# A hybrid encoder step on one core: projections, attention and convolution done per block of 384 rows

## What is computed

```python
xn = rmsnorm(x, norm1_g)
z  = xn @ w_in                      # conv B | conv C | conv h | q | k | v | two gates, 8192 columns
a  = (B * dwconv3_causal(C * h)) @ w_conv_out
q, k = rope(rmsnorm(q)), rope(rmsnorm(k))          # 8 heads, two components of 64
o  = (softmax(q1 k1^T / 8) - lam * softmax(q2 k2^T / 8)) @ v   # chunk-causal; sample rows see 1024 cached keys
b  = (rmsnorm(o) * 0.8) @ w_attn_out
x  = x + (sigmoid(gA) * a + sigmoid(gB) * b) @ w_o
# PEER: per row 8 heads x 16 experts out of 16384, chosen by two top-16 searches over 128 keys
h  = gelu(u[e] . xn2);  x = x + sum_e softmax_weight(e) * h(e) * v[e]       # 128 pairs of rows u, v per row of x
```

## Time and profile before

| | us |
|---|---|
| median of 3 runs | 4466.34 (4462.66 to 4469.68) |
| the profiled execution, its own time | 4468.1 |
| its span | 4466.3 |
| PE busy in the span | 3853.3 (86%) |
| DVE busy | 2490.5 (56%) |
| ACT busy | 1451.2 (32%) |
| POOL busy | 1441.8 (32%) |
| DMA, mean over the span | 295 GB/s, 1318.22 MB |
| granted TensorE clock, mean | 0.967 |

### The profile page before, as it was taken

How to read it: one execution, slowest core, us unless ns; L and a number is a source line. 1 busy time by engine, 2 the same in 40 slices (tenths; PEclk the granted TensorE clock), 3 DMA queues, 4 the chain that set the end, 5 groups by cost and what they waited for, 6 DMA issues and landing times.

```text
span 4466.3 us, 43158 instructions
## 1 busy us (share of the span) xinstructions
PE 3853.3 (86%) x12044; PEld 2048.3 (46%) x12044; DVE 2490.5 (56%) x5795; ACT 1451.2 (32%) x4313; POOL 1441.8 (32%) x1429
## 2 busy tenths in 40 slices
PE   7989999899798899898878998988897777777877
PEld 6657566575455544444434444334453222222222
DVE  4443544435100387767656666666665666666664
ACT  2221312213101244433334444333433333333333
POOL 3112120121000144334444344444444444444442
PEclk9999999999899999999989999999999999999999
DMA  5111011100533699999999999999999999999998
GB/s 176 49 59 48 27 53 47 49 24 21 148 103 111 237 420 415 395 419 403 413 398 419 420 420 419 412 420 420 386 389 417 421 419 420 417 408 413 414 415 343
DMA packets 265946, 1318.22 MB, mean 295 GB/s; under 512 B 28960, under 2 KB 91936, under 8 KB 130400
## 3 DMA queue, kind: packets, MB, share of 16 engines
q0 software_dynamic: 154816, 1116.82, 60.8%
q1 hardware_dynamic: 102000, 175.81, 11.5%
q10 hardware_dynamic: 8880, 22.68, 1.3%
HBM read 1271.17 MB, written 44.06 MB: 294 GB/s over the span
## 4 chain that ended last, share of the span: by engine, by line
DMA 31%; PE 27%; DVE 7%; issue 3%; ACT 3%; POOL 1%; DVEq 1%; ACTq 0%; SPq 0%; POOLq 0%
PE tl_ps L1206 16%; DMA tl_ringx<-in_peer_uv,tl_idx 15%; DMA mix<-in_peer_uv,tl_idx 15%; PE tl_ps L1155 5%; PE tl_ps L1191 3%; PE tl_ps L1167 2%; DVE tl_ringx L1507 2%; DVE mix L1507 2%; ACT tl_dg L1315 1%; PE tl_ps L1135 1%; ACT tl_hw L1308 1%; POOL mix L1096 1%; POOL tl_ringx L1096 0%; ACT tl_hg L1304 0%; DVE tl_oh L1421 0%
## 5 line engine op out<-in xcount | busy, mean ns | idle before, releaser
L1206 PE MATMUL tl_ps<-mix,tl_dg 128*128 128x512 f32 x2296 | 1124.9, 618 | 236.9 <-ACT tl_dg L1315 215.5
L1507 DVE CUSTOM_DVE_ANT_0 mix<-mix,tl_xb 128x1024 f32<-128x1024 f32 x604 | 738.8, 1225 | 570.4 <-DMA mix<-in_peer_uv,tl_idx 554.8
L1096 POOL DMA_INDIRECT mix<-in_peer_uv,tl_idx x604 | 690.9, 1144 | 951.2 <-PE tl_ps L1206 775.3
L1206 PE MATMUL tl_ps<-tl_ringx,tl_dg 128*128 128x512 f32 x1712 | 845.8, 622 | 169.5 <-ACT tl_dg L1315 158.7
L1206 PEld LDWEIGHTS tl_ps<-mix,tl_dg 128*128 128x128 f32 x2296 | 420.2, 194 | 818.4 <-ACT tl_dg L1315 462.4
L1507 DVE CUSTOM_DVE_ANT_0 tl_ringx<-tl_ringx,tl_xb 128x1024 f32<-128x1024 f32 x452 | 552.8, 1225 | 404.0 <-DMA tl_ringx<-in_peer_uv,tl_idx 388.1
L1304 ACT ACTIVATE tl_hg<-tl_hd 128x1 f32<-128x1 f32 x1056 | 213.8, 202 | 1635.7 <-DVE tl_hd L1507 1622.1
L1096 POOL DMA_INDIRECT tl_ringx<-in_peer_uv,tl_idx x452 | 517.0, 1144 | 700.7 <-PE tl_ps L1206 573.9
L1206 PEld LDWEIGHTS tl_ps<-tl_ringx,tl_dg 128*128 128x128 f32 x1712 | 313.3, 194 | 615.2 <-ACT tl_dg L1315 344.9
L1315 ACT ACTIVATE tl_dg<-ident,tl_hw 128x128 f32<-128x128 f32 x1002 | 402.2, 401 | 82.8 <-PE tl_ps L1206 11.7
L1155 PE MATMUL tl_ps<-tl_xr,low 128*128 128x384 f32 (+1 forms) x1280 | 413.0, 454 | 2.8 <-issue 1.7
(11 more groups left out here) (170 smaller groups left out, 3057.2 us busy)
## 6 DMA issues: line engine op xcount, KB each, us to landing
low<-in_wall SPq DMA_DIRECT2D x168, 512.0 KB, 20.7
mix<-in_w_in SPq DMA_DIRECT2D x12, 1024.0 KB, 6.1
low<-in_w_in SPq DMA_DIRECT2D x24, 512.0 KB, 4.1
mix<-in_peer_uv,tl_idx POOLq DMA_INDIRECT x604
sc_rows<-tl_stage ACTq DMA_DIRECT2D x36, 256.0 KB
tl_sch<-sc_rows POOLq DMA_DIRECT2D x18, 512.0 KB, 13.2
tl_ringx<-in_peer_uv,tl_idx POOLq DMA_INDIRECT x452
xn_t<-xnT SPq DMA_DIRECT2D x1, 4224.0 KB, 21.7
```

Source lines behind the costliest of these rows:

```text
L1096: nc.gpsimd.indirect_dma_start(out=ring[q % RING].rearrange("p a d -> p (a d)"), out_offset=None, in_=A["peer_uv"], in_offset=bass.Indirec ...
L1206: last = nc.tensor.matmul(acc[:, h * 512:(h + 1) * 512], dg[:, npe(q) % DIAGS, :], ring[q % RING][:, 1, h * 512:(h + 1) * 512], start=k == ...
L1507: nc.vector.tensor_tensor_reduce(out=ring[q % RING][:, 0, :], in0=ring[q % RING][:, 0, :], in1=xb[:, t % 2, :], scale=1.0, scalar=0.0, op0 ...
```

## The change

`build_attention` is gone. Its work is done in `build_tail`, per block of rows, by a new generator `attend(rb)` on each engine, between that block's neighbours: `attend(0)` and `middle(0)` run in front of slot 0; `attend(1)` is due in slots 0 to 145 and `middle(1)`, now with the convolution of its rows, in 146 to 308; `attend(2)` in 312 to 497 and `middle(2)` with its convolution in 501 to 703. A head's step has 21 positions and a pace (`ATT`: 1.0, 0.78 and 0.98 slots a position), and `SC`, `PJ`, `TW`, `PV`, `TO`, `TQ` are the positions of its scores, projections (of the next head), transposes of weights, products with v and transposes of outputs and heads on PE. ACT's, DVE's and POOL's steps stand some tenths of a position to two positions behind. A projection is now 384 columns wide (q, k and v of one head at once). A block of rows attends to its own keys, which are in SBUF, and to prior ones, which are loaded from memory (`kt`, `v_prompt`; the cache's keys come transposed from the host). Rows that DVE adds are now 111 (`SHARED`: every second slot in 146 to 317, every third in 494 to 701).

```diff
+WRING = 6
 QUAD = 4
 DIAGS = 4
 
 
 BLOCKS = ((0, 3 * P, (0, 1, 2)), (3 * P, 3 * P, (3, 4, 5)), (6 * P, 2 * P + DEC, (6, 7, 8)))
 MID = 56
-START = -140
-PLAN = ((-137.2, 1600, 1600, 7), (-5.5, 1600, 780, 7), (262, 1, 420, 7))
-DVE_TO, DVE_EVERY = 256, 4
+START = -330
+ATT = ((-327.5, 1.0), (-2.5, 0.78), (312, 0.98))
+PLAN = ((-137.2, 1600, 1600, 7), (145, 1, 1750, 7), (499, 1, 1080, 7))
+SC, PJ, TW, PV = (0, 6, 12), (2.2, 8.2, 14.2), (3.4, 9.4, 15.6), (4.8, 10.8, 17)
+TO, TQ, CV = (7.2, 13.2, 19), (10.9, 16.6, 20), (0.6, 6.6, 12.8)
+CONV = (0, 24, 24)
+BASE = (0, MID, 2 * MID + 24)
+SHARED = ((146, 318, 2), (494, 702, 3))
 
 
 def rows_of(t):
...
-            sp.dma_start(keep["kc"][:], group_cols(A["cache_k"], 0)).then_inc(s["ahead"], 16)
-            for kind in range(3):
-                sp.dma_start(keep["w"][kind][:], group_cols(A["w_in"][0], (QCOL, KCOL, VCOL)[kind])).then_inc(s["ahead"], 16)
-            sp.wait_ge(s["ahead"], 64)
+            for k in range(6):
+                src = A["watt"][k] if k < 3 else A["wall"][k - 3]
+                sp.dma_start(keep["low"][:, k * D:(k + 1) * D], src).then_inc(s["ahead"], 16)
...
-def build_attention(nc, A, keep):
...
+def step_at(rb, h, pos):
+
+    first, pace = ATT[rb]
+    return first + ((h + 1) * 21 + pos) * pace
...
+                def project(g, i):
...
+                    for c in range(DC):
+                        yield PJ[i] + 0.1 * c
+                        if c == 0:
+                            if i == 0:
+                                seen = g + 1 if rb == 0 else DC * (1 - par) + 4 * (rb - 1) + g % DC // 2 + 1
+                                pe.wait_ge(s[f"a_in{par}"], 48 * seen)
+                            if j >= 2:
+                                pe.wait_ge(s["qn_d"], j - 1)
+                                pe.wait_ge(s["v_cp"], j - 1)
+                            if rb:
+                                pe.wait_ge(s["ex_d"], done["scores"])
+                        last = nc.tensor.matmul(o, xn[:, c, i * P:i * P + n], w[:, :, c, :], start=(c == 0), stop=(c == DC - 1))
+                    last.then_inc(s["pj_done"], 1)
+                    done["heads"] += 1
...
+                    for i, t in enumerate(tiles):
+                        if h >= 0:
+                            yield step_at(rb, h, SC[i])
+                            score(g, i, (0,) if t == NT else (0, 1))
+                            if rb == 0:
+                                for pos in conv_block(h, i):
+                                    yield step_at(rb, h, pos)
+                            if i:
+                                yield step_at(rb, h, TO[i - 1])
+                                turn_out(g, i - 1)
+                            if t == NT:
+                                yield step_at(rb, h, SC[i] + 1.6)
+                                score(g, i, (1,))
+                        if h + 1 < DC:
+                            for pos in project(g + 1, i):
+                                yield step_at(rb, h, pos)
+                        if h >= 0:
+                            blocks = (key_count(t) + P - 1) // P
+                            yield step_at(rb, h, TW[i])
+                            turn_weights(g, i, 0, blocks if turns(t) == 1 else 4)
+                            if turns(t) == 2:
+                                yield step_at(rb, h, TW[i] + 0.6)
+                                turn_weights(g, i, 4, blocks)
+                        if h + 1 < DC and i == 2:
+                            yield step_at(rb, h, TQ[1])
+                            turn_heads(g + 1, 1)
+                        if h >= 0:
+                            yield step_at(rb, h, PV[i])
+                            weigh_values(g, i)
+                        if h + 1 < DC and i == 1:
+                            yield step_at(rb, h, TQ[0])
+                            turn_heads(g + 1, 0)
+                    if h >= 0:
+                        yield step_at(rb, h, TO[2])
+                        turn_out(g, 2)
+                    if h + 1 < DC:
+                        yield step_at(rb, h, TQ[2])
+                        turn_heads(g + 1, 2)
...
+                    act.wait_ge(s["pj_done"], j + 1)
+                    nc.scalar.copy(Vown[:n, par, i, :], ps[:n, 2 + j % 2, 2 * P:3 * P]).then_inc(s["v_cp"], 1)
+                    if j:
+                        act.wait_ge(s["ss_d"], j)
+                    nc.scalar.activation(sq[:n], ps[:n, 2 + j % 2, 0:2 * P], ACT.Square, scale=HD ** -0.5).then_inc(s["sq_d"], 1)
...
+                    for i, t in enumerate(tiles):
+                        if h >= 0:
+                            if i:
+                                yield step_at(rb, h, TO[i - 1] + 0.2)
+                                keep_out(g, i - 1)
+                            if t == NT:
+                                yield step_at(rb, h, SC[i] + 1.4)
+                                exp_scores(g, i, (0,))
+                                yield step_at(rb, h, SC[i] + 2.9)
+                                exp_scores(g, i, (1,))
+                            else:
+                                yield step_at(rb, h, SC[i] + 1.5)
+                                exp_scores(g, i, (0, 1))
+                            if i == 0 and rb == 0:
+                                yield step_at(rb, h, CV[0] + 1.0)
+                                act.wait_ge(s["f_done"], 3 * h + 1)
+                                if h:
+                                    act.wait_ge(s["u_done"], h)
+                                nc.scalar.copy(Cb[:, 0:nr], ps[:, 6, 0:nr]).then_inc(s["c_done"], 1)
+                        if h + 1 < DC:
+                            yield step_at(rb, h, PJ[i] + 0.9)
+                            keep_value(g + 1, i)
+                        if h >= 0:
+                            for half in range(turns(t)):
+                                yield step_at(rb, h, TW[i] + 0.2 + 0.6 * half)
+                                keep_weights(g, i, half)
+                        if h + 1 < DC and i:
+                            yield step_at(rb, h, TQ[i - 1] + 0.2)
+                            keep_heads(g + 1, i - 1)
+                        if h >= 0:
+                            yield step_at(rb, h, PV[i] + 0.5)
+                            square_out(g, i)
+                    if h >= 0:
+                        yield step_at(rb, h, TO[2] + 0.2)
+                        keep_out(g, 2)
+                    if h + 1 < DC:
+                        yield step_at(rb, h, TQ[2] + 0.2)
+                        keep_heads(g + 1, 2)
+                        yield step_at(rb, h, TQ[2] + 0.6)
+                        store_heads(g + 1)
...
+                    for i, t in enumerate(tiles):
+                        if h >= 0:
+                            if i:
+                                yield step_at(rb, h, PV[i - 1] + 1.8)
+                                norm_out(g, i - 1)
+                            yield step_at(rb, h, SC[i] + 0.6)
+                            row_max(g, i, (0,) if t == NT else (0, 1))
+                            if t == NT:
+                                yield step_at(rb, h, SC[i] + 2.2)
+                                row_max(g, i, (1,))
+                            if rb == 0 and i:
+                                yield step_at(rb, h, CV[i] + 1.1)
+                                conv_product(h) if i == 1 else conv_taps(h)
+                            yield step_at(rb, h, SC[i] + (3.3 if t == NT else 2.4))
+                            difference(g, i)
+                        if h + 1 < DC:
+                            yield step_at(rb, h, PJ[i] + 1.2)
+                            mean_square(g + 1, i)
+                            yield step_at(rb, h, PJ[i] + 2.2)
+                            rotate(g + 1, i)
+                    if h >= 0:
+                        yield step_at(rb, h, PV[2] + 1.8)
+                        norm_out(g, 2)
...
-            steps = [started(middle(rb)) for rb in range(PASSES)] + [started(routing())]
+            steps = [started(part(rb)) for rb in range(PASSES) for part in (attend, middle)] + [started(routing())]
```

More of the change, by code:

```diff
@@ L835, in by_dve @@
 def by_dve(q):
-    return q < DVE_TO and (4 if q < SLOTS else 30) <= q % SLOTS < SLOTS - 4 and q % DVE_EVERY == DVE_EVERY - 1
+    t, k = divmod(q, SLOTS)
+    if not (4 if t == 0 else 30) <= k < SLOTS - 4:
+        return False
+    return any(first <= q < end and q % turn == turn - 1 for first, end, turn in SHARED)
 def ndve(q):
@@ L858, in slot_of @@
         return at / (ahead if at < 0 else rate)
-    for j in range(MID):
+    for j in range(-conv, MID):
         if j == 40:
@@ L1209, in weigh @@
                 last.then_inc(s["used_pe"], 1)
-            steps = [started(middle(rb)) for rb in range(PASSES)]
+            steps = [started(part(rb)) for rb in range(PASSES) for part in (attend, middle)]
             for q in range(START, LAST):
@@ L1341, in _ @@
```

(2 more changed lines are left out.)

1166 lines of the change are left out of this document (560 added, 606 removed).

## The result

The changed kernel takes 4766.5 us (median of 4 runs, 4761.5 to 4773.9) against 4468.0 (4 runs): ratio 1.067, 95% interval 1.065 to 1.069. It is slower, as forecast (4576 us, +2.4%), but by more than twice the forecast, and outside the range of 4310 to 4740.

A forecast was written before the change was run, and what follows sets the result against it. PE was taken to bound slots 0 to 703, gathers the rest: 771 + 466 + 230 + 638 + 33 + 569 + 273 + 638 + 41 + 906 + 11 = 4576 us; own range 4450 to 4700, over the cases 4310 to 4740.

The forecast's parts named there:

- First dot, 771: In front of the slots: first dot at 44.6 + 357 + 370 = 771 us, 771 earlier; bounds 720 and 830.
- The two middle stretches, 671 and 679: Slots 146 to 311 and 498 to 703: PE's work 638 us each, plus 33 and 41 at 0.2 a slot.
- The gathers alone, 906 and 11: From slot 704 on: 352 slots at the gathers' 2.574 us, 906 us as now, plus 11 at the end.
- The waits, 230 and 273: Attention slots 0 to 145 and 312 to 497: PE waits on ACT's same-iteration steps and exps, 503 us in all.
- Plain couplings: Attention slots: 84 and 91 iterations where PE waits for ACT's step and diagonal chain, mean 1.75 us, 147 and 159.
- Waits behind an exp: Attention slots: table loads and exps hold PE 5.3 us, or 2.4 with half a projection between; 83 and 114 us.
- VectorE joins in: Rival, chance 0.17: DVE's softmax and rotation add waits in the attention slots, 503 becomes 650; 4723 us.
- Transfers: Rival, chance 0.04: DMA sets the slots throughout, with PE under 2.8 us a slot; 3878 us.
- PE's own work, 466 and 569: Slots 0 to 145 and 312 to 497: PE's matmuls, 452 and 552 us at gapless prices, become 466 and 569.
- the clock of 0.97: Slots 0 to 703: PE's granted clock, taken from the kernel before, turning its priced work into 2311 us.
- two signs: Forecast wrong if PE's diagonal waits in the attention slots total under 390 us, or the first dot is beyond 830.
- absorbed: Rival, chance 0.29: ACT runs ahead in the attention slots, so waits are mostly absorbed, under 393 us; 4334 us.

The follow-up runs named there:

- experiment 1: Changed kernel with ScalarE doing slot q's gelu, gate and diagonal ahead of its attention and middle steps of the iteration; 4660.5 us, ratio 1.042.
- experiment 6: Changed kernel with TensorE doing slot q - 1's product in iteration q, behind its steps, instead of slot q's; 4441.2 us, ratio 0.992 to the kernel before.
- experiment 8: Kernel of experiment 6 with the exponentials replaced by a Square without a table, masked scores 0, so no softmax; 4364.6 us, ratio 0.976.
- experiment 3: Changed kernel with two zero-weight matmuls of 512 columns on TensorE before the diagonal wait in 230 attention iterations; 4822.4 us, ratio 1.078.
- experiment 4: Changed kernel with block 1's attention also in front of the gathers, its middle still at slots 145 to 311; 4831.7 us, ratio 1.080.
- experiment 5: Kernel of experiment 4 with three zero-weight matmuls of 512 columns ahead of each of 21 projection waits for an exp; 4785.4 us, ratio 1.070.
- experiment 2: Changed kernel with the attention's exponentials replaced by a Square needing no table of its own, masked scores 0, so no softmax; 4611.3 us, ratio 1.032.
- experiment 9: Kernel of experiment 6 with projections 0.8 of a position later, weight transposes and product with V 0.2 to 0.5 later; 4418.2 us, ratio 0.990.
- experiment 7: Kernel of experiment 6 with every fourth row of the attention stretches (66 more) added by VectorE; 4452.1 us, ratio 0.995.
- experiment 10: Kernel of experiment 9 with every fourth row of the attention stretches (66 more) added by VectorE; 4429.7 us, ratio 0.991.

## Why the forecast had the sign right and the size wrong

**First dot, 771.** It came at 779.9. Both of its parts are right as well: the first matmul of the merge (L978) starts at 413.2 us where 401.6 was forecast, and from there to the dot it is 367 us where 370 was.

**The two middle stretches, 671 and 679.** They took 652 and 683. Right; here the granted clock is 0.98 and 0.96, as assumed.

**The gathers alone, 906 and 11.** 931, 14 more; DMA's share is 0.99.

**The waits, 230 and 273.** They were 215 and 245. The mechanism is shown by experiments 1 and 6, which take the coupling away from either side. That the sum is so near is in part luck, since its two parts miss in opposite directions. Plain couplings were forecast at 84 and 91 waits of 1.75 us, 147 and 159 us; there were 61 and 74 of 1.5 us, 92 and 114. Waits behind an exp were forecast at 83 and 114 us; with those at L798 and L776 they came to 113 and 117. "VectorE joins in" is refuted, since all waits stayed under 503 and PE's own on DVE were 2.6 us in block 1 and 8.8 in block 2. Transfers did not set the pace (DMA's share 0.62 and 0.64).

**PE's own work, 466 and 569: the step that failed.** The prediction took the prices of gapless stretches and "the clock of 0.97" for stretches into which it had itself just put 503 us of waits. PE was busy 541 and 715 us, 75 and 146 more. With the other terms that is the miss: 9 + 75 - 15 - 19 + 146 - 28 + 4 + 14 = 186, and 4762.7 - 4576 = 187. These 221 us are of two kinds, and the trace's clock tells them apart. The low clock cost 50 and 97 us; the forecast's 0.97 held 14 and 17 of that, so 116 are clock that it left out. The other 106 are under-pricing: at full clock PE's work is 491 and 619 us, where the forecast had 452 and 552. Experiments 6 and 8, at higher clocks and with fewer waits, both give 478 and 607, so this count hangs little on the clock of the run. Of the 106 some 62 are in attention's scores, transposes and products with V (261 us for 199), 34 in the slots' products (596 for 562) and 9 in the projections. That the waits bring the low clock is shown by experiment 3 (78 us less for the same work with PE kept busy in the same waits) and by the pair 4 and 5.

The Trainium skill (TensorE: Matmul & The Clock Gate, HAM oscillation — how this bites in real kernels) describes just this, matmuls that start cold again after each wait, for a kernel that waits on DMA. The traces agree: 7.99 us against 5.43 for the same eight matmuls. The prediction did not weigh that page.

**The exponentials.** Forecast as the dearest waits for their number, 5.3 us behind most of them, 83 and 114 us in all. Experiment 2 puts the table loads that they bring at 155 us, 86 of it as waits and 69 as PE's busy time. In the changed kernel's first attention stretch (records, busy us, mean ns):

```profile
L1247 ACT ACT_TABLE_LOAD x27 | 34.6, 1283 | 0.5
L1058 ACT ACT_TABLE_LOAD x24 | 30.8, 1283 | 22.5 <-DVE tl_nb L1418 22.1
```

The loads are 1283 ns each, as forecast. The Trainium skill (ScalarE: Activation LUTs, What ACT_TABLE_LOAD costs) has 1.38 us of drain beside each; in block 2 an exp starts at 2619.99, 1.29 us after its load began at 2618.70, so the drain does not show here either.

**What would have shown it wrong.** The prediction named two signs. The first dot passed. The other, waits on diagonals under 390 us in the attention slots, came true: they were 182 + 198 = 380. Yet this does not make the rival "absorbed" right, which had the same bound (393) for all waits: those were 460, and the time was 430 us above its 4334. The sign counted diagonals alone, where the term of 503 held every wait, also those at L798 and L776. And no sign named PE's busy time or its clock, the term that failed.

Where the change goes wrong, then, is mostly in the order within an iteration. With that mended (experiments 6 and 9) the same restructuring is 0.8 and 1.0% faster than the kernel before. Open remains what sets the 4.0 and 4.15 us a slot that attention still takes in experiment 9. Experiment 7 excludes the amount of PE's work. The waits left there are 95 us on diagonals, 59 at L798 and L776 for exps, and smaller ones on DVE; which of these chains comes first was not shown, and banks of its own for the projection were not tried.

## What to carry to other kernels

A wait put into TensorE was paid for twice here: its own length, 460 us in all, and the work behind it at half clock, another 147 us. When work of one engine and its consumer is laid into the slots of a software pipeline, look in which iteration each of the two stands; one iteration of distance on the consumer's side was worth 325 us, for an edit of three lines. Before moving work off an engine, check that it has no waits: in experiments 7 and 10 the saved work was given back whole. And when waits are put into a forecast, price the work between them anew, clock and short pieces both.
